# Part buffers of the experts and the dense stage moved out of the ring's last slot, and the gather as 32 fp32r products on high and low halves of the tokens

## What is computed

```python
def _swiglu(h, wg, wu, wd):
    return (jax.nn.silu(h @ wg) * (h @ wu)) @ wd

def _moe(h, w_router, wg, wu, wd):
    logits = (t @ w_router).astype(jnp.float32)
    top_v, top_i = lax.top_k(logits, TOP_K)
    top_w = jax.nn.softmax(top_v, -1)
    gates = jnp.sum(jax.nn.one_hot(top_i, N_EXPERTS) * top_w[..., None], axis=1)
    for e in range(N_EXPERTS):
        y = y + gates[:, e:e + 1] * _swiglu(t, wg[e], wu[e], wd[e])
```

## Time and profile before

| What | Value |
|---|---|
| Median of 3 runs | 1942.04 us (1940.99 to 1943.09) |
| The profiled execution | 1941.47 us |
| Its span, first to last instruction | 1939.2 us |
| Mean granted TensorE clock | 0.988 |
| TensorE busy | 1871.1 us, 96% of the span |
| VectorE busy | 1401.3 us, 72% |
| ScalarE busy | 1089.8 us, 56% |
| HBM read | 528.20 MB, 274 GB/s over the span |

### The profile page before, as it was taken

The page is one execution under the profiler, slowest core; times in us unless marked ns, Lnnn a source line. Parts: engine busy times, 40 slices in busy tenths (PEclk is TensorE's granted clock), DMA queues, the critical chain, the costliest instruction groups (busy, mean ns, idle before and its releaser), DMA issues.

```text
span 1939.2 us, 24178 instructions
## 1 busy us (share of the span) xinstructions
PE 1871.1 (96%) x9097; PEld 1406.5 (73%) x9097; DVE 1401.3 (72%) x1420; ACT 1089.8 (56%) x1031; POOL 29.9 (2%) x53
## 2 busy tenths in 40 slices
PE   4999999999989999998999999999999999999995
PEld 1885554677868855546888888888888888888884
DVE  1575853644566677536988888879889798898886
ACT  2453332444444433325777777777677776777773
POOL 1000010000000000100000000000000000000000
PEclk9999999999989999999999999999999999999998
DMA  9766444576565653525999999999999999999992
GB/s 352 261 214 211 151 149 161 199 260 217 196 217 211 234 180 132 179 87 205 355 369 325 369 342 352 365 327 366 338 354 368 339 354 345 349 367 344 349 366 108
DMA packets 231135, 531.71 MB, mean 274 GB/s; under 512 B 7832, under 2 KB 10448, under 8 KB 231072
## 3 DMA queue, kind: packets, MB, share of 16 engines
q1 hardware_dynamic: 227024, 520.78, 74.2%
q0 software_dynamic: 3168, 9.80, 1.6%
q10 hardware_dynamic: 880, 0.27, 0.1%
HBM read 528.20 MB, written 2.62 MB: 274 GB/s over the span
## 4 chain that ended last, share of the span: by engine, by line
PE 95%; DVE 2%; issue 1%; DMA 1%; ACT 0%; ACTq 0%; POOL 0%; DVEq 0%; POOLq 0%
PE ps L853 20%; PE ps L854 20%; PE ps L855 20%; PE ps L783 16%; PE ps L840 2%; PE ps L817 2%; PE ps L804 2%; PE ps L806 2%; PE ps L807 2%; PE ps L1241 2%; PE ps L1269 1%; DMA arena<-in_cv_w 1%; PE ps L1109 1%; PE ps L962 0%; PE ps L993 0%
## 5 line engine op out<-in xcount | busy, mean ns | idle before, releaser
L2275 DVE TENSOR_TENSOR arena_r<-ring,arena_r 128x2048 fp32r<-128x2048 f32 x224 | 512.4, 2292 | 96.8 <-ACT arena_r L1411 95.2
L1411 ACT ACTIVATE arena_r<-ring 128x2048 fp32r<-128x2048 f32 x225 | 431.1, 1916 | 84.3 <-PE ps L855 84.3
L853 PE MATMUL ps<-arena_r 128*128 128x512 f32 x1128 | 446.7, 396 | 8.2 <-DVE arena_r L1775 6.4
L854 PE MATMUL ps<-arena_r 128*128 128x512 f32 x1128 | 441.1, 391 | 0.0
L855 PE MATMUL ps<-arena_r 128*128 128x512 f32 x1128 | 364.1, 390 | 0.0
L2275 DVE TENSOR_TENSOR ring_r<-ring,ring_r 128x2048 fp32r<-128x2048 f32 x113 | 259.0, 2292 | 42.3 <-ACT ring_r L1411 40.2
L853 PEld LDWEIGHTS ps<-arena_r 128*128 128x128 f32 x1128 | 213.1, 189 | 55.4 <-issue 8.3
L855 PEld LDWEIGHTS ps<-arena_r 128*128 128x128 f32 x1128 | 212.8, 189 | 45.3
L854 PEld LDWEIGHTS ps<-arena_r 128*128 128x128 f32 x1128 | 213.0, 189 | 44.0
L1411 ACT ACTIVATE ring_r<-ring 128x2048 fp32r<-128x2048 f32 x113 | 216.5, 1916 | 45.1 <-PE ps L855 45.1
L853 PE MATMUL ps<-ring_r,arena_r 128*128 128x512 f32 (+1 forms) x592 | 235.4, 398 | 2.4 <-DVE arena_r L2270 1.7
(11 more groups left out here) (238 smaller groups left out, 1905.3 us busy)
## 6 DMA issues: line engine op xcount, KB each, us to landing
ring<-in_moe_w_gate SPq DMA_DIRECT2D x113, 1024.0 KB, 5.1
ring<-in_moe_w_up SPq DMA_DIRECT2D x113, 1024.0 KB, 7.4
ring<-in_moe_w_down SPq DMA_DIRECT2D x112, 1024.0 KB, 6.4
ring<-in_w_in SPq DMA_DIRECT2D x28, 2048.0 KB, 8.2
ring<-in_w_mod SPq DMA_DIRECT2D x24, 2048.0 KB, 8.8
ring<-in_ffd_w_gate SPq DMA_DIRECT2D x5, 2048.0 KB, 13.3
ring<-in_ffd_w_up SPq DMA_DIRECT2D x5, 2048.0 KB, 7.8
ring<-in_ffd_w_down SPq DMA_DIRECT2D x5, 2048.0 KB, 7.7
```

The source lines that it names most:

```text
L853: mm(o_, hi, w_hi[:, n], start=start, stop=False)
L854: mm(o_, hi, w_lo[:, n], start=False, stop=False)
L1411: act_(e_part(j)[0], raw_part(j), ACT.Copy).then_inc(part_hi, 1)
L2275: V.tensor_tensor(w_lo, raw_part(j), w_hi.bitcast(F32), ALU.subtract).then_inc(part_lo, 1)
```

## The change

Seven things are edited. (1) `e_part(j)` for `j % 3 == 0` goes to the arena: its high half to columns 8192 to 10240, its low half to 20992 to 23040. (2) `hg_hi`, `hg_lo`, `yd_hi`, `yd_lo` go to the ring's last slot, 1024 columns each. (3) In the dense stage the two part buffers in the ring's last slot move to arena columns 13824 to 17920 from the fifth part on. (4) The first 14 blocks of `dT_lo` move to the ring's last slot. (5) The tokens are kept as a high and a low half: ScalarE writes `htok_hi` in fp32r, VectorE subtracts it from PSUM into `htok_lo`, which lies in `z` for group 0 and in `hT` for group 1; VectorE instead of ScalarE frees the banks. (6) The gather is 32 fp32r products, high and low for each of the 16 before, and `S` becomes an fp32r tile at its old place. (7) `mrow2` moves by 512 columns.

```diff
-        hg_hi, hg_lo = arena_r[:, 8192:9216], arena_r[:, 9216:10240]
-        yd_hi, yd_lo = arena_r[:, 20992:22016], arena_r[:, 22016:23040]
+        htok_hi = arena_r[:, 17408:17408 + G * D]
+        hg_hi, hg_lo, yd_hi, yd_lo = (ring_r[:, i * D:(i + 1) * D] for i in range(4))
+        S_r = nc.alloc_sbuf_tensor_at("S_r", [P, G * P], F32R, offset=nc.lookup_mloc(hT).addr + 4 * 1024)
+        htok_lo = (nc.alloc_sbuf_tensor_at("htok_lo0", [P, D], F32R, offset=nc.lookup_mloc(z).addr),
+                   nc.alloc_sbuf_tensor_at("htok_lo1", [P, D], F32R, offset=nc.lookup_mloc(hT).addr))
...
-        dT_hi, dT_lo = arena_r[:, 6144:6144 + 22 * T], arena_r[:, 6144 + 22 * T:17408]
+        dT_hi, dT_lo = arena_r[:, 6144:6144 + 22 * T], (arena_r[:, 6144 + 22 * T:13824], ring_r[:, 0:14 * T])
...
             if phase_of(j) == "dense":
-                return split_part(s)
+                b = split_part(s)
+                if s < 2 and j - D0 >= DPARTS:
+                    b = [arena_r[:, 13824 + (2 * s + h) * PART:13824 + (2 * s + h + 1) * PART] for h in range(2)]
+                return b
...
             s = j % EPARTS
-            b = ring_r[:, 0:2 * EHALF] if s == 0 else arena_r[:, (s - 1) * 2 * EHALF:s * 2 * EHALF]
+            if s == 0:
+                return arena_r[:, 8192:8192 + EHALF], arena_r[:, 20992:20992 + EHALF]
+            b = arena_r[:, (s - 1) * 2 * EHALF:s * 2 * EHALF]
...
-                        ins = mm(o_[:, j * P:(j + 1) * P], htok[:, g * D + (4 * h + j) * P:g * D + (4 * h + j + 1) * P],
-                                 S[:, g * P:(g + 1) * P], start=(g == 0), stop=(g == 1))
+                        c = (4 * h + j) * P
+                        mm(o_[:, j * P:(j + 1) * P], htok_hi[:, g * D + c:g * D + c + P], S_r[:, g * P:(g + 1) * P],
+                           start=(g == 0), stop=False)
+                        ins = mm(o_[:, j * P:(j + 1) * P], htok_lo[g][:, c:c + P], S_r[:, g * P:(g + 1) * P],
+                                 start=False, stop=(g == 1))
...
+                def token_high(g):
+                    for h in range(2):
+                        await_product(sc, "htok", g, h)
+                        act_(htok_hi[:, g * D + h * 512:g * D + (h + 1) * 512], bank(("htok", g, h)),
+                             ACT.Copy).then_inc(htok_high, 1)
...
+            def token_low(g, h):
+
+                hs = slice(h * 512, (h + 1) * 512)
+                await_product(dv, "htok", g, h)
+                st.next(htok_high)
+                free(V.tensor_tensor(htok_lo[g][:, hs], bank(("htok", g, h)), htok_hi[:, g * D + h * 512:g * D + (h + 1) * 512].bitcast(F32),
+                                     ALU.subtract), "htok", g, h)
...
                 modulated("h2T", 24, 32, 1)
+                if l:
+                    token_low(0, 0), token_low(0, 1)
...
             st.done(V.tensor_tensor(R(DIFF, 2), R(V2, 2), R(V1, 2), ALU.subtract), gate_arg)
+            token_low(1, 0)
             st.next(gate_exp)
...
                 st.done(V.tensor_tensor(EG(WT + 16 * n), GE(TOP1), GE(TOP2), ALU.add))
+            token_low(1, 1)
             await_product(dv, "rank")
```

More of the change, by code:

```diff
@@ L415, in build @@
         diag2 = arena[:, 6144:8192]
-        mrow2 = arena[:, 17408:17920]
+        mrow2 = arena[:, 17920:18432]
         sil_d, act_d = arena[:, 18432:19456], arena[:, 19456:20480]
@@ L419, in build @@
         at[0] = 17408
-        htok = carve(G * D)
+        carve(G * D)
         sil, act = carve(512), carve(1024)
@@ L494, in build @@
             sem(n) for n in ("diag_ready", "gate_arg", "gate_exp", "mask_ready", "sel_ready", "flag_ready", "y_ready", "y_sum"))
-        scattered, gate_col, sums_zeroed = sem("scattered"), sem("gate_col"), sem("sums_zeroed")
+        scattered, gate_col, sums_zeroed, htok_high = (sem(n) for n in ("scattered", "gate_col", "sums_zeroed", "htok_high"))
         dve_step, act_step, pool_step = sem("dve_step"), sem("act_step"), sem("pool_step")
@@ L567, in turned_to @@
             f0, fn = FCHUNKS[i]
+            if buf is dT_lo:
+                buf, f0 = buf[f0 >= 8 * P], f0 % (8 * P) if f0 < 8 * P else f0 - 8 * P
             return buf.rearrange("p (f t) -> p f t", t=T)[:, f0 // P:(f0 + fn) // P, g * P:(g + 1) * P]
@@ L1191, in _, with down_low @@
                     ys = {(g, n): claim("Y", g, n) for g in range(G) for n in range(2)}
+                    def down_low(f, g):
+                        f_ = (f if f < 8 else f - 8) * T + g * P
+                        return dT_lo[f >= 8][:, f_:f_ + P]
                     def dense_down(f, groups):
@@ L1198, in dense_down @@
                             inss = split_mm([(ys[g, n], slice(512 * n, 512 * n + 512)) for n in range(2)],
-                                            dT_hi[:, fs], dT_lo[:, fs], *early_part(j), f == 0, f == FF_D // P - 1)
+                                            dT_hi[:, fs], down_low(f, g), *early_part(j), f == 0, f == FF_D // P - 1)
                             if f == FF_D // P - 1:
@@ L1297, in experts @@
                                 for g in range(G):
-                                    mm(o_[:, 256:257], S[:, g * P:(g + 1) * P], wsel[:, g:g + 1], start=(g == 0),
+                                    mm(o_[:, 256:257], S_r[:, g * P:(g + 1) * P].bitcast(F32), wsel[:, g:g + 1], start=(g == 0),
                                        stop=(g == G - 1), skip_group_check=True)
                                 for g in range(G):
-                                    ins = tr(o_[:, g * P:(g + 1) * P], S[:, g * P:(g + 1) * P], ident)
+                                    ins = tr(o_[:, g * P:(g + 1) * P], S_r[:, g * P:(g + 1) * P].bitcast(F32), ident)
                                 e_full(ins, "ST")
@@ L1589, in _ @@
                 if l:
-                    for h in range(2):
-                        take(htok[:, h * 512:(h + 1) * 512], ("htok", 0, h))
+                    token_high(0)
                 modulated("h2T", 24, 32, 1)
@@ L1603, in _ @@
                 if l:
-                    for h in range(2):
-                        take(htok[:, D + h * 512:D + (h + 1) * 512], ("htok", 1, h))
+                    token_high(1)
                     st.next(gate_arg)
```

4 lines of the change are left out of this document (2 added, 2 removed).

## The result

| What | Before | After |
|---|---|---|
| Median | 1942.02 us (1940.24 to 1943.13, 11 runs) | 1947.49 us (1945.72 to 1949.01, 11 runs) |
| The profiled execution, and its span | 1941.47, 1939.2 us | 1949.01, 1946.7 us |
| Mean granted TensorE clock | 0.988 | 0.981 |
| TensorE busy | 1871.1 us | 1878.3 us |

The changed kernel is slower by 5.5 us: the ratio is 1.0028, with an interval from 1.002 to 1.0037. The forecast was 1943.7. The time lies in the stated range (1933 to 1958.5), 3.8 us above the forecast and outside the 0.2% within which the prediction called two times the same.

What follows compares the result with a forecast made beforehand. TensorE was taken to bound the kernel. Experts +4.6, dense stage -2.5, gather 0 and start -0.5 sum to +1.6; with the profiled 1941.5 and 0.6 to the median, 1943.7 us, range 1933 to 1958.5 for 8 in 10.

Steps and rivals of the forecast that it cites:

- TensorE's stream sets the end: Whole kernel: 95% of the time to the last instruction is TensorE, so a change counts by its effect on TensorE's stream.
- Experts +4.6: Eight experts: gate and up parts get slower, down parts gain 0.4 us an expert; together +4.6 us, bounds +1.6 and +5.6.
- the scatter: Scatter products in the experts, both operands outside the arena afterwards: 227 to 234 ns each, at most -0.5 us, taken as 0.
- Rival 4: All products: places cost nothing after the move and only the routing counts, 1941.5 us; chance 0.05.
- Dense stage -2.5: Dense stage: all parts but the first two leave the ring and run at the settled arena price, -2.5 us.
- Gather in the loop 0: Eight gathers in the experts: 32 fp32r products at 112 ns, set by the weight load, 0 us; +2.0 kept for the range.
- Rivals 2 and 5: Gather's 128-column fp32r products: 2, two entries of 112 ns, 1974 us, chance 0.08; 5, 81 ns, 1935 us, chance 0.05.
- The start -0.5: Before the first expert: routing +1.1 us and first gather -1.6 us, in sum -0.5 us.
- The routing's +1.1: Routing before the first expert: of VectorE's four added subtractions two are hidden, the others cost +0.4 and +0.7 us.
- two fp32 passes over 128 columns then outlast the weight load. One pass would not: First gather, at nearly 1.2 GHz: 5.44 us would become 3.6 to 3.8 with one pass, -1.6 us.
- The end 0: From the last scatter to the last norm: the prediction had no gain there, forecast 0.
- the main case: The forecast of 1943.7 us itself, chance 0.65; its range reaching above the same-time band gave 0.16 of the chance for slower.

## Why the prediction was right, and where it was not

1. **TensorE's stream sets the end**: right. The chain is 95% TensorE's in both, and each difference in the table above is one in that stream or in VectorE's routing and norm ahead of and behind it.
2. **Experts +4.6**: 4.7 in the traces, from the prices that the prediction took (2.81 and 2.72 a part). The reading under it, "fast when both of its operands lie in the arena, and slow when one of them lies elsewhere, whichever it is", was wrong all the same: what counts is whether the two addresses leave the same remainder by 256. In the layout of the kernel before the two readings part only for a pair with both operands outside the arena, which the prediction said no row shows. That pair, the scatter, was the sign: 229 ns in the mean and 227 in the median of 65 products. The term for it was 0, with -0.5 as the bound. That the price held was luck of the layout: the change turned a difference of 96 (234.3 ns) into one of 160 (234.1). With the arena behind the ring the same move of buffers leaves the period where it was (123.73 against 123.69).
   The Trainium skill's rule, "SBUF — State Buffer" (Who interferes with whom), by which TensorE's two reads are independent, agrees with the traces when the remainders are equal (227.2 to 227.5 ns in three layouts), and does not account for the product when they differ (230 to 234). Whether it is these reads that meet is not shown. So neither the rule nor the reading that I put in its place had the cause. Rival 4, places that cost nothing, is what the two kernels with the arena behind the ring show.
3. **Dense stage -2.5**: -2.96, by the same price. At the place of the earlier trace rows 24 products now take 5.44 us whichever part they are of, 227 ns each, as these rows of the changed kernel's timeline show:

```profile
393.15 0.39 PE L863 MATMUL ps<-arena_r 128*128 128x512 f32 x1
...
398.59 0.39 PE L863 MATMUL ps<-arena_r 128*128 128x512 f32 x1
```

4. **Gather in the loop 0**: right: 3.69 us, and an expert's period with the new gather alone is 125.37 against 125.36. Rivals 2 and 5 fall.
5. **The start -0.5**: the step that failed; it was +5.3 in the traces without the low clock ahead of the logits (0.9 + 1.6 + 2.8). The routing's +1.1 was right in kind and size (+0.9). In runs, the new gather alone cost 3.8 us, where its terms sum to -0.5. What failed is "two fp32 passes over 128 columns then outlast the weight load. One pass would not". At the lower clock the load takes longer too (333 ns recorded against 192, and an entry of 8 columns takes the same 0.2 us as one of 128), so an entry is 213 ns in either form. And the prediction let the low stretch last as long as before, when the change itself lengthened the idle time ahead of it from 2.61 to 3.50 us. It lasted 13.7 to 17.1 us in all five profiled kernels that have the new gather without products of zeros in front of it, and 3.4 in all six that have the old gather without them. Whether the longer idle time or the one-pass products keep it low was not separated. Filling the idle time ended it in the kernel with four products of zeros; in the trace with seven the clock was low for 23.9 us though there was no such idle time, so idle time is not the only way to a low clock, and the cause of the length stays open.
6. **The end 0**: -1.1. VectorE starts the last norm earlier in the kernels with the new gather (0.84 us behind the first scatter product in the one with the gather alone) and not in the one with the buffers alone (1.98). Ahead of that operation VectorE's program has a branch around a second pass of the experts. Why it gets past it sooner no run shows; it stays open.

The forecast's terms sum to +1.6, those of the traces to +5.9 without the two stretches of low clock. The gap of 4.3 is the start (+5.8) and the experts (+0.1), less the end (1.1) and the dense stage (0.5): one mis-sized step. The chance of 0.30 for slower held that outcome as the upper part of the main case, for reasons of the experts' price; it came by another way, so the time fell into the range partly by luck.

## What to carry to other kernels

Before a change moves operands between buffers, take the addresses of both operands of the matmul and the remainder of their difference by 256. Here 96 bytes of padding in the kernel before were worth 16.5 us (ratio 0.9911), three times what the change cost. Nothing that ran was faster than this kernel and the two with the arena behind the ring that are level with it (1925.2 to 1925.5 us). Where a step ahead of TensorE gets longer, price the work behind it at the lower clock, weight loads included, and for longer than the last such stretch lasted. Work put into an idle gap must be shorter than the gap at the lower clock too, or it costs more than the gap.

## What the runs showed of the chip that I had not expected

- In long streams an fp32r product of 512 columns takes 227 ns from start to start where the addresses of its two operands in the partition leave the same remainder by 256, and 230 to 234 ns at differences of 64, 96, 128, 160, 192 and 224 bytes, over more than a thousand products each. That holds whichever of the two buffers streams, and 256 bytes are as good as 0. What in the chip makes it is not shown.
- At the lower of the two granted clocks a stream of load and product keeps one pace for 8 and for 128 columns, as at the upper one, so the load sets it, as far as these rows tell: 213 ns an entry, for 128 columns in fp32 and in fp32r and for 8 in fp32, against 110 to 112. The recorded load goes from 192 to 333 ns.
- The granted clock can fall while TensorE is busy: at 898.6, 1.2 us into products of zeros and 12.7 us after its last idle time above 0.21 us. Only one run of that kernel has a trace; the times and the mean clock (0.980, against 0.987 to 0.989) suggest that 3 of its 12 runs are alike.
